# Turning 32x32 blocks on VectorE in place of one of two products per level in the delta rule's triangular inverse

## What is computed

```
decay = jnp.where(tril, jnp.exp(jnp.where(tril, diff, 0.0)), 0.0)
k_beta = kc * bc[..., None]
lower = jnp.where(strict, jnp.einsum('bhnik,bhnjk->bhnij', k_beta, kc) * decay, 0.0)
t_inv = lax.linalg.triangular_solve(eye + lower, eye, left_side=True, lower=True, unit_diagonal=True)
u = t_inv @ v_beta
w = t_inv @ (k_beta * jnp.exp(gc)[..., None])
```

## Time and profile before

| | |
|---|---|
| time, median of 3 runs | 1750.21 us (1748.21 to 1751.4) |
| span of the profiled execution | 1743.7 us, that is 6.5 us under that median |
| TensorE busy, VectorE busy | 1536.5 us (88%), 875.3 us (50%) |
| ScalarE busy, GpSimd busy | 659.4 us (38%), 149.6 us (9%) |
| mean granted TensorE clock | 0.947 |
| read from device memory | 414.04 MB |

### The profile page before, as it was taken

The page is one execution under the profiler, slowest core; times in us unless marked ns, Lnnn a source line. Parts: engine busy times, 40 slices in busy tenths (PEclk is TensorE's granted clock), DMA queues, the critical chain, the costliest instruction groups (busy, mean ns, idle before and its releaser), DMA issues.

```text
span 1743.7 us, 35055 instructions
## 1 busy us (share of the span) xinstructions
PE 1536.5 (88%) x14790; PEld 1321.3 (76%) x14790; DVE 875.3 (50%) x1263; ACT 659.4 (38%) x869; POOL 149.6 (9%) x188
## 2 busy tenths in 40 slices
PE   9999999999999999999999999799998564656568
PEld 8999899988989989998899799698874232323234
DVE  5765466645665556664587688956641010101011
ACT  5445355435444435543566744525441000000001
POOL 5800000000000000000106011130010000000000
PEclk9999999999999999999999999999999678787879
DMA  7765566774744757664454343002899999999995
GB/s 251 242 218 176 188 168 193 225 258 149 262 143 155 249 181 205 192 194 165 134 161 155 97 152 117 26 27 76 314 391 410 431 432 431 430 429 430 431 431 250
DMA packets 238133, 417.16 MB, mean 239 GB/s; under 512 B 13698, under 2 KB 213929, under 8 KB 228009
## 3 DMA queue, kind: packets, MB, share of 16 engines
q1 hardware_dynamic: 237817, 414.59, 66.0%
q10 hardware_dynamic: 176, 0.53, 0.1%
HBM read 414.04 MB, written 1.05 MB: 238 GB/s over the span
## 4 chain that ended last, share of the span: by engine, by line
issue 47%; PE 42%; DVE 4%; POOL 4%; ACT 3%; DMA 1%; DVEq 0%; SPq 0%; POOLq 0%; ACTq 0%
PE bank L429 4%; PE bank L431 4%; PE bank L430 4%; PE bank L1919 2%; PE bank L445 2%; PE bank L447 2%; PE bank L446 2%; PE bank L1075 1%; PE bank L1077 1%; PE bank L457 1%; PE bank L761 1%; PE bank L1076 1%; PE bank L458 1%; PE bank L459 1%; DVE cy L1433 1%
## 5 line engine op out<-in xcount | busy, mean ns | idle before, releaser
L250 DVE TENSOR_TENSOR w_lo<-w_raw,w_hi 128x2048 fp32r<-128x2048 f32 (+2 forms) x178 | 400.3, 2252 | 249.9 <-ACT w_hi L243 246.3
L243 ACT ACTIVATE w_hi<-w_raw 128x2048 fp32r<-128x2048 f32 (+2 forms) x178 | 334.0, 1881 | 152.4 <-DMA w_raw<-in_ffn_w_down_dram 61.7
L429 PE MATMUL bank<-h_hi,w_hi 128*128 128x256 f32 x1168 | 325.3, 279 | 7.0 <-DVE h_lo L639 3.7
L430 PE MATMUL bank<-h_lo,w_hi 128*128 128x256 f32 x1168 | 324.4, 278 | 0.0
L431 PE MATMUL bank<-h_hi,w_lo 128*128 128x256 f32 x1168 | 324.4, 278 | 0.0
L429 PEld LDWEIGHTS bank<-h_hi,w_hi 128*128 128x128 f32 x1168 | 220.3, 189 | 8.4 <-issue 8.3
L2799 PE MATMUL bank<-w_exp_four,xeT 128*32 128x256 f32 x1600 | 133.3, 502 | 99.0 <-DMA w_exp_four<-in_w_up_dram 59.2
L430 PEld LDWEIGHTS bank<-h_lo,w_hi 128*128 128x128 f32 x1168 | 220.4, 189 | 0.0
L431 PEld LDWEIGHTS bank<-h_hi,w_lo 128*128 128x128 f32 x1168 | 220.3, 189 | 0.0
L2799 PEld LDWEIGHTS bank<-w_exp_four,xeT 128*32 128x32 f32 x1600 | 67.0, 142 | 164.4 <-issue 87.5
L2932 ACT ACTIVATE sg<-bank 128x256 f32<-128x256 f32 x16 | 6.1, 384 | 391.4 <-PE bank L2799 391.4
(11 more groups left out here) (537 smaller groups left out, 3130.9 us busy)
## 6 DMA issues: line engine op xcount, KB each, us to landing
w_exp_four<-in_w_up_dram SPq DMA_DIRECT2D x13, 4096.0 KB, 33.3
w_exp_four<-in_w_down_dram SPq DMA_DIRECT2D x13, 4096.0 KB, 33.6
w_exp_four<-in_w_gate_dram SPq DMA_DIRECT2D x12, 4096.0 KB, 33.3
w_raw<-in_ffn_w_gu_dram SPq DMA_DIRECT2D x88, 512.0 KB, 5.1
w_raw<-in_w_in_dram SPq DMA_DIRECT2D x54, 512.0 KB, 4.6
w_mod<-in_w_mod_dram SPq DMA_DIRECT2D x24, 1024.0 KB, 6.9
w_raw<-in_ffn_w_down_dram SPq DMA_DIRECT2D x44, 512.0 KB, 4.2
w_raw<-in_mem_w_kv_dram SPq DMA_DIRECT2D x32, 512.0 KB, 4.6
```

The source lines that it names most:

```text
L243: e.activation(whi[slot][:, 0:w], raw[slot][:, 0:w], ACT.Copy).then_inc(S["hi_ready"], 1)
L250: e.tensor_tensor(wlo[slot][:, 0:w], raw[slot][:, 0:w], whi[slot][:, 0:w].bitcast(F32), ALU.subtract).then_inc(S["lo_ready"], 1)
L429: e.matmul(dst, whi[slot][:, lo:hi_], bh[:, k, :], start=begin, stop=False)
L430: e.matmul(dst, whi[slot][:, lo:hi_], bl[:, k, :], start=False, stop=False)
```

## The change

It touches the inverse and the start of it in `masks`. (1) At levels 1 to 4 the product `Ym` with `TT` and its subtraction from `TT` are gone; instead VectorE transposes the updated `Tm` into `TT`, in one instruction (`turned_blocks`, L1900 in the new numbering), which turns each 32x32 block in its place. The inverse is block diagonal with blocks of at most 32 up to level 4, so this is the same matrix. (2) Level 5 keeps its one product and its subtraction (now L1952). (3) In `masks`, `TT` is no longer built from `LT` by two operations but turned from `Tm`. (4) The waits are split: `y_part` waits for `Tm` alone and no longer for `TT`, the products of `t_part` wait for the turn, and GpSimd's first cut waits for `LT` alone.

```
             for t_ in range(TT):
...
-                t = dve.do(lambda e, t_=t_: e.tensor_tensor(f4(TT_, t_), f4(LT, t_), lv, ALU.mult), t, *free)
-                t = dve.do(lambda e, t_=t_: e.tensor_tensor(f4(TT_, t_), idb, f4(TT_, t_), ALU.subtract), t)
-                self.T_ready[t_] = [t_T, t]
+                self.TT_ready[t_] = [self.turned_blocks(t_, t_T, *free)]
+                self.L_ready[t_] = [t]
+                self.T_ready[t_] = [t_T]
                 yield
...
+        def turned_blocks(self, t_, *w):
+            flat = lambda v_: v_[:, t_, :, :].rearrange("p s j -> p (s j)")
+            return dve.do(lambda e: e.transpose(flat(self.TT), flat(Tm)), *w)
...
-            lvl = {t_: level_part(1, t_, *T_ready[t_], *(free if self.grp else ())) for t_ in range(TT)}
+            lvl = {t_: level_part(1, t_, *self.L_ready[t_], *(free if self.grp else ())) for t_ in range(TT)}
...
             def t_part(l, t_):
-                T_ready[t_] = []
-
                 if l < 5:
-                    tp = small_mm(bk[2 + t_], f4(TT_, t_), f4(Ym, t_), ty[t_], *bfree[2 + t_])
-                tp2 = small_mm(bk[t_], f4(Ym, t_), f4(TT_, t_), ty[t_])
-                if l < 5:
-                    bfree[2 + t_] = [dve.do(lambda e: e.tensor_tensor(f4(Tm, t_), f4(Tm, t_), bank3(2 + t_), ALU.subtract), tp)]
-                    T_ready[t_] += bfree[2 + t_]
-                bfree[t_] = [dve.do(lambda e: e.tensor_tensor(f4(TT_, t_), f4(TT_, t_), bank3(t_), ALU.subtract), tp2)]
-                T_ready[t_] += bfree[t_]
+                    tp = small_mm(bk[2 + t_], f4(TT_, t_), f4(Ym, t_), ty[t_], *TT_ready[t_], *bfree[2 + t_])
+                    bfree[2 + t_] = T_ready[t_] = [
+                        dve.do(lambda e: e.tensor_tensor(f4(Tm, t_), f4(Tm, t_), bank3(2 + t_), ALU.subtract), tp)]
+                    TT_ready[t_] = [turned_blocks(t_, tp, *T_ready[t_])]
+                else:
+                    tp = small_mm(bk[t_], f4(Ym, t_), f4(TT_, t_), ty[t_], *TT_ready[t_])
+                    bfree[t_] = [dve.do(lambda e: e.tensor_tensor(f4(TT_, t_), f4(TT_, t_), bank3(t_), ALU.subtract), tp)]
```

More of the change, by code:

```diff
@@ L1875, in masks @@
             idb = id64[:, :].rearrange("p (a j) -> p a j", a=1).broadcast_to((P, NS, CH))
-            lv = lev[:, 0:1, :].broadcast_to((P, NS, CH))
-            self.T_ready = {}
+            self.T_ready, self.TT_ready, self.L_ready = {}, {}, {}
             for t_ in range(TT):
@@ L1896, in masks @@
                 bfree[b] = [t]
-            self.masked = self.T_ready[0] + self.T_ready[1]
+            self.masked = self.TT_ready[0] + self.TT_ready[1]
+        def turned_blocks(self, t_, *w):
+            flat = lambda v_: v_[:, t_, :, :].rearrange("p s j -> p (s j)")
+            return dve.do(lambda e: e.transpose(flat(self.TT), flat(Tm)), *w)
         def inverse(self, bk, bfree, turn_bank, hooks, scaled_free, *free):
-            TT_, T_ready = self.TT, self.T_ready
+            TT_, T_ready, TT_ready, turned_blocks = self.TT, self.T_ready, self.TT_ready, self.turned_blocks
             def turn_heads(src, tiles, *after):
```

## The result

The changed kernel takes 1744.19 us at the median of eight runs (1733.7 to 1747.92); the kernel before, also of eight runs, 1751.03 (1748.21 to 1754.62). The ratio is 0.9947, with a 95% interval from 0.9929 to 0.9964: about 9.3 us less. The two medians differ by less, 6.8 us, and the two means by 8.9, so the size is known to some 3 us only. Forecast were 8.2 less, 1742.0 us, and a range of 1738.5 to 1747. The measured median lies in the range, 2.2 us above the forecast. The profiled execution took 1747.92 us over a span of 1746.2, which is 2.5 us more than the span of before, although the kernel is faster. That has to be explained first.

A forecast was written before the change was run, and what follows sets the result against it. TensorE was taken to bound the outer two edited stretches, VectorE the middle, bytes the tail from 1230 us. Terms: -0.3 - 2.8 + 1.1 - 6.9 + 0.7 = -8.2 us, giving 1742.0 us, range 1738.5 to 1747.

The forecast's parts named there:

- What bounds each stretch, and that the gain arrives at the end: TensorE bounds 1058-1081.5 and 1139-1187, VectorE between; time won before 1230 us should reach the end whole.
- TensorE's products, 0.93 each: Sixteen products of 0.93 us go: three in the first stretch, five in the middle, eight in the last.
- A turn of 0.91 us: VectorE's 512-column transpose in level updates costs 0.91 us (0.635 to 1.27), making a pair 1.52, 0.32 more.
- Masks, 0.3 and 0.6: Turning in `masks`: 0.3 us less before 1058 (0 to 1.2), 0.6 back ahead of group 1's `rr` (0.2 to 0.9).
- The middle stretch, 1.1 more: 1081.5 to 1139: five pairs 1.6 more, `qf` 0.6 back, `masks` 0.6 back, clock 0.7; 1.1 us more.
- the clock's term of 0.7 (0 to 1.6): Middle stretch: longer TensorE gaps lower its clock, 0.7 us more, kept small as TensorE isn't the bound there.
- the 0.6 that `qf` was to give back: Middle stretch: `qf` operations start before ScalarE's roots are ready; VectorE arriving later loses less, 0.6 us back (0 to 1.0).
- the slower rival: Turns collide with GpSimd's cuts; at 2.5 us a turn the kernel is 3 slower, 1753 us; chance 0.05.
- The last stretch, 6.9 less: 1139 to 1187: eight products save 7.45 us, of which 0.5 to 0.6 is lost at `rr`; net 6.9 less.
- The wait for `rr` in the second round: Group 1, last stretch: the weight split ahead of `rr` makes TensorE wait about 0.5 us; 1.2 lost with long turn.
- The clock in the last stretch: Rival: a wait for `rr` or `Tm` lets TensorE's clock fall for 10 us, 4 us back, 1746; chance 0.08.
- The 0.7 for what I couldn't follow: Allowance of 0.7 us on the dear side for GpSimd's cuts behind `y_part` and ScalarE's place at the last level.

The follow-up runs named there:

- the products kept: Changed kernel, but TensorE still computes the second product of levels 1 to 4, unread, and the turn waits for it; ratio to before 0.9969.
- the filled kernel: Changed kernel plus eight unread 128x128 matmuls at each of three long TensorE waits; ratio to before 0.9915, median of six runs 1739.12 us.
- the second profile of the changed one: Changed kernel run and profiled once more, unedited; ratio to before 0.995.

## Why the prediction was right, and where only by balance

The likeliest case came true: 8.2 forecast, 9.4 measured by the marks, 9.3 and 8.8 by the two ratios, 6.8 by the medians. That the sum is so near is in part luck. By the marks the parts are off by 1.0 more gained before the first product, about 0.5 more from there to group 1's first, 0.9 less behind it, and 0.7 that was put by and not needed. By its own steps:

- **What bounds each stretch, and that the gain arrives at the end.** Right. The sixth `rr` comes 9.4 us earlier from `masks` on and the total is 9.3 and 8.8 shorter; the tail itself can be read to some 4 us only.
- **TensorE's products, 0.93 each.** Right: 4.67 for five in the first stretch (the prediction, which cut it at 1081.5, counted three and left two to the wait for `vb`), and with the products kept both outer stretches go back. But the gain of the first stretch was taken for one that stays, and with the clock's falls it mostly doesn't (79.4 with the products kept, 79.1 and 78.5 without).
- **A turn of 0.91 us.** Too dear by 0.2, from a row of another form; still inside the bounds 0.635 and 1.27. A pair of update and turn takes 1.40 and not 1.52, 0.2 more than two subtractions instead of 0.32.
- **Masks, 0.3 and 0.6.** Too small: 1.3 and 1.5, both above their ranges (0 to 1.2, 0.2 to 0.9). For the first I took the end at which one wait counts, but what both tiles save arrives almost whole at the first product. Of the second, 0.6 is GpSimd's.
- **The middle stretch, 1.1 more.** The size was near and the terms were wrong. From the first product to group 1's the forecast was 2.8 less and 1.1 more, 1.7 less; measured are 1.9 and 2.5 less. But the clock's term of 0.7 (0 to 1.6) was some 4: the filled kernel is 3.3 us shorter there than the second profile of the changed one although its operations of `cy` and `qf` took 2.4 more beside cuts, which makes 5.7, and 1.5 of that is the fall which the kernel before has too. This is an estimate: it takes the 2.4 as if all of it stood on the path. And the 0.6 that `qf` was to give back became 3.1: the two `qf` operations take 1.3 instead of 2.4, two of `cy` 0.48 instead of 1.49. Two errors of 3.3 and 2.5 nearly cancelled. The step that failed is "TensorE isn't the bound there", by which a slow clock seemed cheap: while the clock is low the products between two of VectorE's updates take longer than VectorE's other work. In the changed kernel VectorE stood 2.19 us for them; in the kernel before it did not wait at that place.

```profile
1107.20 2.58 DVE L1433 SCALAR_TENSOR_TENSOR cy<-pad,vcol,cy 128x256 f32<-128x256 f32 x6
1111.98 0.69 DVE L1948 TENSOR_TENSOR Tm<-Tm,bank 128x512 f32<-128x512 f32 x1 [2.19 <-PE bank L1922]
1112.77 0.71 DVE L1900 STREAM_TRANSPOSE TT<-Tm 128x512 f32<-128x512 f32 x1
1113.40 0.65 DVE L1948 TENSOR_TENSOR Tm<-Tm,bank 128x512 f32<-128x512 f32 x1
1114.16 0.71 DVE L1900 STREAM_TRANSPOSE TT<-Tm 128x512 f32<-128x512 f32 x1
1115.55 1.29 DVE L1799 TENSOR_TENSOR qf<-qf,sq 128x512 f32<-128x512 f32 x2 [0.68 <-ACT sq L1794]
```

- **Why `qf` took 2.4.** The prediction gave two readings, ScalarE's roots and, under the slower rival, GpSimd. It is GpSimd: when the cut (1114.00) is over before the pair starts (1115.55), the pair takes 1.29, and it still waits for the roots.
- **The last stretch, 6.9 less.** It was 6.0. The wait for `rr` in the second round was 1.05 and not 0.5 to 0.6:

```profile
1165.41 0.68 DVE L2047 TENSOR_TENSOR rr<-bank,gb 128x512 f32<-128x512 f32 x1
1166.12 1.68 DVE L2049 TENSOR_TENSOR rr<-vb,rr 128x512 f32<-128x512 f32 x1
```

```profile
1165.99 2.94 POOL L1932 TENSOR_TENSOR AT<-LT,lev 128x512 f32<-128x512 f32 x2 [2.86 <-PE bank L1922]
```

  This is the slower rival's collision, at another instruction. `rr<-vb,rr` of 0.69 started 0.13 us behind the start of a cut and took 1.68. The rest, about 0.4, I can't place.
- **The slower rival.** A turn does not collide: the one at 1114.16 lies wholly beside the cut of 1114.00, and takes 0.71 as all twenty do. The Trainium skill (SBUF — State Buffer, Who interferes with whom) has the rule of which both halves show here: a VectorE instruction with two SBUF inputs and a GpSimd one that reads SBUF can't run together, and whichever starts first holds the other for its whole length. The `cy`, `qf`, `Tm` and `rr` operations end 0.2 to 0.6 us behind the cut they met; the turn, with one input, doesn't wait. One input alone is not what spares it, though. The first two operations on `cy` (L1432, `TENSOR_SCALAR`) read one tile, `pad`, and a column `vcol`; beside a cut of the kernel before the pair takes 1.09 and not 0.60, its first operation 0.83 instead of 0.35, and the same happens once in each profile of the changed kernel.

```profile
1081.56 1.09 DVE L1432 TENSOR_SCALAR cy<-pad,vcol 128x256 f32<-128x256 f32 x2 [2.98 <-ACT pad L1415]
```

```profile
1080.96 2.85 POOL L1929 TENSOR_TENSOR AT<-LT,lev 128x512 f32<-128x512 f32 x2 [9.75 <-PE bank L1919]
```

- **The clock in the last stretch.** It did not fall: it is 1.00 from 1148.7 to 1230.
- **The 0.7 for what I couldn't follow** was not needed.

## What to carry to other kernels

When TensorE stops being the bound of a stretch, its clock becomes a cost of its own: look for the waits that lengthen, and price the work behind them at half speed as part of the chain between two engines. Unread products in the shadow of such waits gave 3.7 us here. When an edit shifts GpSimd's work by a microsecond or two, look at which of VectorE's operations from SBUF it now meets: here they moved 2 us of VectorE's time in either direction, and what of that reaches the total was not tried by an edit of its own. A gain in a stretch that TensorE bounds is not won before the next stretch, which another engine bounds, has been passed. And an effect of half a per cent is read between marks inside the edited region, which repeat within 0.1 to 0.6 us, and not from spans, which differed by 7 to 11 us for one kernel.

## What the runs showed that was not expected

- The same 128x256 matmuls run at 0.1134 or 0.1178 us, start to start, at a granted clock of 1.00, for many microseconds at a time (0.1134 from 250 to 350 us in the first profile of before and the second of after, 0.1178 in the other two); which it is differs between executions of one kernel. The cause is open.
- A turn of 32x32 blocks over 512 columns takes 0.71 us, hardly more than an elementwise operation of 0.69; read in an order eight elements apart it takes 1.10.
- What stays open: what makes the clock fall behind one wait of 2.2 us and not behind another, and what a kernel would take with neither the clock's falls nor the collisions. The filled kernel still has 2.4 us of them in the middle stretch and 1.0 at `rr`.
